# Differential norm: the variance taken inside ScalarE's logarithm and on GpSimd, and the first head's loads spread over slots

## The reference, cut to what matters

```python
def _rmsnorm(x, g):
    y = x * lax.rsqrt(jnp.mean(x * x, axis=-1, keepdims=True) + EPS)
    return y * g

def _diff_attention(q, k, v, lam, lambda_init, g_subln):   # 4 heads, 2048 rows, 64 values
    def block(args):                                       # 128 queries
        qb, t0 = args
        sc = jnp.einsum('bqhmd,bkhmd->bhmqk', qb, k) * scale
        p = jax.nn.softmax(jnp.where(allowed, sc, -jnp.inf), axis=-1)
        a = p[:, :, 0] - lam * p[:, :, 1]
        return jnp.einsum('bhqk,bkhe->bqhe', a, v)
    o = _from_blocks(lax.map(block, (_to_blocks(q), starts)))
    return _rmsnorm(o, g_subln) * (1.0 - lambda_init)
```

## Time and profile before

| | |
|---|---|
| median of three runs | 2027.23 us (2026.43 to 2027.46) |
| the profiled execution | 2035.85 us |
| its span, first to last instruction | 2034.1 us |
| PE / PEld / DVE / ACT / POOL busy | 91% / 77% / 64% / 53% / 30% of the span |
| granted TensorE clock, mean | 0.96 of full speed |
| differential stage | about 1450 us to 1822 us of the span |

### The profile page before, as it was taken

One profiled execution on the slowest core, in us unless ns is written; L12 is line 12 of the kernel. 1 busy time (PEld: TensorE's weight loads), 2 busy tenths in 40 slices (PEclk: granted clock), 3 DMA queues, 4 the chain that ended last, 5 costly groups with the idle time before them and its releaser, 6 DMA issues.

```text
span 2034.1 us, 34303 instructions
## 1 busy us (share of the span) xinstructions
PE 1856.4 (91%) x11552; PEld 1557.3 (77%) x11552; DVE 1305.7 (64%) x2685; ACT 1085.4 (53%) x2406; POOL 603.7 (30%) x542
## 2 busy tenths in 40 slices
PE   6999998889898989898989899999689999979998
PEld 6999998767777777777777787777466666657886
DVE  7705888267676767676767683434577778754454
ACT  6321122266666666666666673434478989962221
POOL 0000000034343434343434350101246666650000
PEclk9999999699999999999999999999599999998999
DMA  6423112200101010101010102413801414016442
GB/s 217 108 68 109 67 67 83 68 6 7 26 5 26 5 26 5 26 5 26 5 26 5 26 18 78 154 53 111 185 1 27 89 27 92 7 54 230 174 145 83
DMA packets 121837, 129.05 MB, mean 63 GB/s; under 512 B 81936, under 2 KB 94992, under 8 KB 120464
## 3 DMA queue, kind: packets, MB, share of 16 engines
q1 hardware_dynamic: 121744, 127.86, 21.6%
HBM read 85.89 MB, written 41.94 MB: 63 GB/s over the span
## 4 chain that ended last, share of the span: by engine, by line
PE 68%; DVE 15%; issue 7%; ACT 6%; POOL 3%; DMA 1%; SPq 0%; DVEq 0%; POOLq 0%; ACTq 0%
PE ps L665 7%; PE ps L619 6%; PE ps L651 5%; PE ps L621 5%; PE ps L620 5%; PE ps L606 4%; PE ps L607 4%; PE ps L608 4%; DVE small L1507 4%; PE ps L897 3%; PE ps L899 3%; PE ps L898 3%; DVE ring L1387 2%; PE ps L848 2%; POOL ring_r L1625 2%
## 5 line engine op out<-in xcount | busy, mean ns | idle before, releaser
L1625 POOL TENSOR_TENSOR ring_r<-ring,sp_hi 128x512 fp32r<-128x512 f32 (+1 forms) x320 | 358.2, 1119 | 855.5 <-DVE sp_hi L1390 855.5
L665 PEld LDWEIGHTS ps<-v,ring 128*128 128x128 f32 x2176 | 284.9, 192 | 52.6 <-issue 17.4
L665 PE MATMUL ps<-v,ring 128*128 128x65 f32 x2176 | 284.9, 270 | 16.3 <-ACT ring L1047 9.8
L1035 ACT ACTIVATE ring<-ps 128x512 f32<-128x512 f32 (+1 forms) x320 | 170.5, 533 | 228.1 <-PE ps L642 135.4
L619 PE MATMUL ps<-ht_hi,w_hl 128*128 128x512 f32 x448 | 199.2, 445 | 25.5 <-DVE sb_s L1417 24.9
L606 PE MATMUL ps<-w_hl,ht_hi 128*128 128x256 f32 x768 | 214.1, 279 | 0.5 <-DVE w_hl L1245 0.3
L607 PE MATMUL ps<-w_hl,ht_hi 128*128 128x256 f32 x768 | 213.9, 279 | 0.0
L608 PE MATMUL ps<-w_hl,ht_lo 128*128 128x256 f32 x768 | 213.9, 278 | 0.0
L1651 POOL TENSOR_TENSOR p<-p 128x1024 f32<-128x1024 f32 (+4 forms) x96 | 164.8, 1728 | 164.6 <-ACT p L1157 164.4
L1387 DVE SCALAR_TENSOR_TENSOR ring<-ring,ps 128x512 f32<-128x512 f32 (+1 forms) x320 | 191.4, 598 | 27.1 <-ACT ring L1040 26.0
L1507 DVE TENSOR_REDUCE small<-ps 128x1 f32<-128x1024 f32 (+4 forms) x192 | 168.7, 905 | 49.3 <-PE ps L806 29.0
(11 more groups left out here) (182 smaller groups left out, 3944.3 us busy)
## 6 DMA issues: line engine op xcount, KB each, us to landing
w_raw<-in_w_narrow SPq DMA_DIRECT2D x18, 512.0 KB, 3.8
xb<-in_x SPq DMA_DIRECT2D x16, 512.0 KB, 4.2
gate_scr<-ring SPq DMA_DIRECT2D x64, 128.0 KB, 1.8
cs<-rot_scr SPq DMA_DIRECT2D x32, 256.0 KB, 3.9
gb<-gate_scr SPq DMA_DIRECT2D x16, 512.0 KB, 3.6
yb<-y_scr SPq DMA_DIRECT2D x16, 512.0 KB, 4.5
xr<-in_x SPq DMA_DIRECT2D x16, 512.0 KB, 4.3
out_y<-ob SPq DMA_DIRECT2D x16, 512.0 KB, 2.9
```

The source lines that it names most:

```text
L665: mm = pe.matmul(ps[:, 4 + i % 2, j * (HD + 1):(j + 1) * (HD + 1)], ring[:, 4 + i % 2, j * P:(j + 1) * P], v1[:, kb, :], start=True, stop= ...
L1625: nc.gpsimd.tensor_tensor(ring_r[:, i % 4, j0 * P:], ring[:, i % 4, j0 * P:], sp_hi[:, i % 4, j0 * P:].bitcast(F32), ALU.subtract).then_in ...
```

## The change

In the differential norm, DVE keeps the sum of squares (L1557) and no longer makes the variance (L1561). ACT's logarithm reads the sum itself, with scale 1/64 and eps as a per-partition bias column (`eps_col`, set once by a DVE memset at the start, behind the semaphore `eps_ok`). POOL makes the variance for the Newton step by a `tensor_scalar` at the head of `df_norm`. The waits move with it: DVE now waits before the sum of batch b until POOL and ACT have read the sum of batch b - 1 (`df_var`, `df_ln`); ACT waits for the sum and for POOL's Newton step of batch b - 1 (`df_nr`); POOL waits for the sum.

On SP, `load_df_v(0)` moves to slot 27, and the four parts of `load_qk(0)` are issued in slots 28 to 31, one part to a slot, so that the stores of memory row steps 26, 27 and 28 stand between them.

```diff
--- before.py
+++ after.py
@@ -154,6 +154,7 @@
         small = sb("small", [P, 256], F32)
         invf = small[:, 0:1]
         minus_lam = small[:, 1:2]
+        eps_col = small[:, 7:8]
         qk_scale = sb("qk_scale", [P, 1], F32)
         w_raw = sb("w_raw", [P, DC * WIDE], F32)
         with ExitStack() as a:
@@ -305,6 +306,7 @@
             sem("df_" + n) for n in ("oc", "ot", "ob", "sq", "ss", "var", "ln", "y0", "nr", "r", "g", "yok"))
         df_pad = [sem("df_pad0"), sem("df_pad1")]
         pool_go = sem("pool_go")
+        eps_ok = sem("eps_ok")
         lam_ch, lam_e = sem("lam_ch"), sem("lam_e")
         wo_in, wo_hi_ok, wo_lo_ok, gpost_in = [sem("wo_in0"), sem("wo_in1")], sem("wo_hi_ok"), sem("wo_lo_ok"), sem("gpost_in")
         o_xr, o_out = ([sem(f"o_{n}{u}") for u in range(2)] for n in ("xr", "out"))
@@ -437,10 +439,12 @@
                 sp.wait_ge(df_lo, f + 1)
                 sp.dma_start(qk_scr[h, 1, :, cols], lo_tmp[:, f % 2, :].bitcast(F32)).then_inc(qk_out[f % 2], 16)
 
-            def load_qk(h):
+            def load_qk(h, only=None):
 
                 u, half = h % 2, S // 2
                 for part, dst, row, first in ((0, df_k, 2 * DQ, 0), (0, df_q, 0, half), (1, df_k, 2 * DQ, half), (2, df_q, 0, 0)):
+                    if only not in (None, (part, row)):
+                        continue
                     cols = slice(first, first + half)
                     for r, hl in enumerate((0, 1, 0) if dst is df_k else (0, 0, 1)):
                         sp.dma_start(dst[u][r * DQ:(r + 1) * DQ, :, cols].bitcast(F32),
@@ -472,12 +476,14 @@
                         store_qk(f)
 
 
+                if slot == X_SLOT[-1] + 2:
+                    load_df_v(0)
                 if slot == X_SLOT[-1] + 3:
                     for u in range(2):
                         sp.wait_ge(qk_out[u], 32 * NT // 2)
                     sp.wait_ge(x_pj, len(X_ITEMS))
-                    load_qk(0)
-                    load_df_v(0)
+                if 3 <= slot - X_SLOT[-1] < 7:
+                    load_qk(0, ((0, 2 * DQ), (0, 0), (1, 2 * DQ), (2, 0))[slot - X_SLOT[-1] - 3])
 
 
             for u in range(2):
@@ -1187,9 +1193,16 @@
             def df_root(s):
                 if s % 2 or not 0 <= s < N_SL:
                     return
-                rsqrt_of(df_tmp(4, 4), df_tmp(8, 4), df_tmp(12, 4), df_var, s // 2 + 1, df_ln, df_y0)
+                b = s // 2
+                act.wait_ge(df_ss, b + 1)
+                if b:
+                    act.wait_ge(df_nr, 4 * b)
+                nc.scalar.activation(df_tmp(8, 4), df_tmp(0, 4), ACT.Ln, scale=1.0 / HD, bias=eps_col).then_inc(df_ln, 1)
+                act.wait_ge(df_ln, b + 1)
+                nc.scalar.activation(df_tmp(12, 4), df_tmp(8, 4), ACT.Exp, scale=-0.5).then_inc(df_y0, 1)
 
             act.wait_ge(m_y, N_MT)
+            act.wait_ge(eps_ok, 1)
             for u in range(2):
                 act.wait_ge(qk_out[u], 32 * len(X_D) // 2)
             for s in range(N_SL + 6):
@@ -1261,6 +1274,7 @@
                 src = (0, 1, 2, 0, 3, 4)[k]
                 nc.vector.tensor_copy(dst[:], cst[:, src, :]).then_inc(const_ok, 1)
             nc.vector.memset(v1[:, :, HD:HD + 1], 1.0).then_inc(lam_ch, 1)
+            nc.vector.memset(eps_col, EPS).then_inc(eps_ok, 1)
             nc.vector.memset(qk_scale[0:2 * DQ, :], -DQ ** -0.5).then_inc(df_scale, 1)
             nc.vector.memset(qk_scale[2 * DQ:P, :], 1.0).then_inc(df_scale, 1)
             lam4 = lam_in.rearrange("p (a b d) -> p a b d", a=2, b=2)
@@ -1552,13 +1566,12 @@
                 if s % 2 or not 0 <= s < N_SL:
                     return
                 b = s // 2
-                ss, var = df_tmp(0, 4), df_tmp(4, 4)
+                ss = df_tmp(0, 4)
                 dve.wait_ge(df_sq, b + 1)
+                if b:
+                    dve.wait_ge(df_var, b)
+                    dve.wait_ge(df_ln, b)
                 nc.vector.tensor_reduce(ss, osq[:], AXX, ALU.add).then_inc(df_ss, 1)
-                dve.wait_ge(df_ss, b + 1)
-                if b:
-                    dve.wait_ge(df_nr, 4 * b)
-                nc.vector.tensor_scalar(var, ss, 1.0 / HD, EPS, ALU.mult, ALU.add).then_inc(df_var, 1)
 
             for u in range(4):
                 dve.wait_ge(m_yout[u], 16 * N_MT // 4)
@@ -1653,8 +1666,10 @@
             def df_norm(b):
                 var, y0, tmp, r = df_tmp(4, 4), df_tmp(12, 4), df_tmp(16, 4), df_tmp(20, 4)
                 a = acc[:, b % 2]
+                pool.wait_ge(df_ss, b + 1)
+                nc.gpsimd.tensor_scalar(var, df_tmp(0, 4), 1.0 / HD, EPS, ALU.mult, ALU.add).then_inc(df_var, 1)
+                pool.wait_ge(df_var, b + 1)
                 pool.wait_ge(df_y0, b + 1)
-                pool.wait_ge(df_var, b + 1)
                 pool.sem_inc(pool_go, 1)
                 nc.gpsimd.tensor_tensor(tmp, y0, y0, ALU.mult).then_inc(df_nr, 1)
                 pool.wait_ge(df_nr, 4 * b + 1)
```

## The result

The change makes the kernel faster: 2012.26 us (2009.79 to 2014.84, five runs) against 2027.46 (2026.43 to 2032.51, five runs). The ratio is 0.9918, with a 95% interval from 0.9904 to 0.9932; 0.0082 of 2027.46 is 16.6 us, where 17.4 was forecast; the two medians lie 15.2 apart. The profiled execution took 2012.26 us, with a span of 2010.2.

The account below looks back on a forecast made before the run. DVE's variance, held behind POOL's instruction, was taken to keep ACT and PE waiting in odd differential iterations. ACT's wait -14.7, clock -3.1, POOL's variance +0.4 sum to -17.4 us: 2027.23 becomes 2009.8, so 2010, range 2002 to 2019.

Parts of the forecast that it names:

- The mechanism: Differential stage: DVE's variance, 0.17 us of work, stands behind POOL's running instruction 14 times, 2.12 us in the median.
- L1561 leaves DVE: Differential stage, odd iterations: removing DVE's variance saves ACT's wait of 1.05 us in each of 14 batches, -14.7 us.
- The lower clock goes with the hole: Two odd iterations at granted clock 0.87 keep 2.4 GHz once the hole goes: 1.55 us each, -3.1 us.
- What takes L1561's place: On DVE, the sum and minima follow at once and no other instruction is held; nothing moves.
- POOL's new variance: POOL's differential norm: 0.38 us more a batch, with room for it; on the path only at stage end, +0.4 us once.
- POOL has the room: POOL, busy 7.23 of 11.2 us in an odd iteration, can take the variance's 0.38 us a batch.
- The logarithm: ACT's logarithm with scale and bias is the same four-column instruction: adds nothing, bounds 0 and 14 x 0.2 us.
- The new waits on DVE: DVE's sum waiting until POOL and ACT have read the previous one: 2.15 us to spare, cost 0.
- Rival D: Slower: DVE's sum waits for a late POOL, 4.7 us late in all 14 batches, +6 us to 2033; chance 0.04.
- The loads: First differential head's loads, spread between memory-row stores on SP: 0 us, the last store's landing staying 1.58 us.
- rival E: Last memory-row store queued behind the fourth load part: up to +4 us, 2014; counted inside the forecast's 0.65 chance.
- The odd iterations: Differential stage: odd iterations take 10.1 to 10.5 us with PE busy nearly throughout; above 10.8 with ACT's waits elsewhere means wrong.
- rival B: Odd iterations: ACT becomes the bound and keeps 0.7 us idle; only -6.3 us, no clock won, 2021; chance 0.13.

Follow-up runs that it names:

- e3: The kernel before the change, with the variance still on DVE but made by four one-column instructions instead of one four-column one; 2011.65 us, ratio 0.9917 to before.
- e4: The changed kernel plus a four-column variance at its old place on DVE, whose result nobody reads; 2026.19 us, ratio 0.9981 to the kernel before.
- e10: The kernel before the change, with ACT's root (logarithm and exponential) moved behind its next exponentials and copy; 2032.76 us, ratio 1.0013 to before.
- e5: The changed kernel without the eps bias column in ACT's logarithm, eps staying in the Newton step; 2012.20 us, ratio 0.9915 to the kernel before.
- e2: The kernel before the change, with only SP's loads spread as in the changed kernel; 2031.14 us, ratio 1.0003 to before.
- e9: The changed kernel, with the memory step's two-column tensor_scalar on DVE made as two one-column instructions; 2011.07 us, ratio 0.9901 to the kernel before.

## Why the prediction was right

**The mechanism was right.** POOL's running instruction holds DVE's four-column `tensor_scalar`. It is taken off (after), made narrow (e3), or put back (e4), and the time follows each time. The Trainium skill (SBUF — State Buffer, Who interferes with whom) says that issue order decides who blocks; the two batches of e4 agree, 0.22 us when DVE is 0.16 ahead and 2.09 when it is 0.28 behind.

**"L1561 leaves DVE", -14.7: the place was wrong, the size nearly right.** The term was priced by ACT's wait for the variance, as the wait that ends last. e10 takes that wait away and wins nothing that helps; e4 gives ACT no such wait and loses the gain again. The price is PE's wait for the copy behind the hold: 17.8 us in 14 batches, 1.27 each, and in e3, which adds only three short instructions on DVE, the eleven odd iterations at full clock fall by 1.31 in the mean. The prediction showed that wait in one batch, 1.39 us, and did not add it up. The two waits differ by 0.2 us a batch, and after does not collect all of the larger one: its stretch is 1.8 us longer than e3's. Of that 0.5 is the bias column (e5); of the rest, 1.0 goes with POOL's longer norm, as the rows under its term show. So two errors, 3.1 too little (17.8 - 14.7) and about 1.8 not taken off, partly cancelled, and that is luck.

**"The lower clock goes with the hole", -3.1: the size nearly right, the reason not shown.** Iterations 9 and 17 took 13.0 us at 0.87 before, and take 10.10 and 10.80 at 1.00; PE's busy time in these two windows falls by 1.64 and 1.66 us, 3.3 of the 4.42 in the stretch. By the stretch's own bounds the two fell by 2.92 and 2.11 us, the other eleven odd ones by 1.17 in the mean, so the clock gave back some 2.7 us, not 3.1. But a hole does not bring the low clock by itself. In before, ten other odd iterations were held for 1.85 to 2.36 us and none of them was at the low clock; the prediction compared with the one short hole alone. In e10 s = 9 and 17 have the same two waits of PE as before in their first six microseconds, 0.34 us and then 1.26 or 1.27, and run at 1.00. In e4 the clock falls in s = 11 and 19 in place of 9 and 17. All ten profiles without the 14 or 9 holds have the full clock over the whole stretch, so the change did win this term; what decides whether a held iteration loses the clock stays open.

**What takes L1561's place: nothing, right.** The sum keeps its 0.42 us, and all 64 of L1541, one column each, take 0.263 to 0.274 us, as in the earlier trace rows.

**POOL's new variance, +0.38 a batch and +0.4 at the end: right there, but it costs elsewhere too.** The chain at the end of the stage, to be laid beside the earlier trace rows:

```profile
1792.40 2.35 POOL p L1664
...
1794.83 0.20 POOL small L1670
...
1796.68 0.62 POOL acc L1690
...
1798.23 0.33 SPq L525
```

From the variance to the first Newton instruction, 1795.23, it is 0.40 us; from the end of the difference to SP's store 3.48 against 2.95 (1821.28 - 1818.33). "POOL has the room" was read from an average. Late in s = 13 and 19 POOL runs without a pause: the norm, then the weight split, then the next difference, which therefore reaches PE later. PE's turn in s = 13, in after and then in e3, where DVE makes the variance:

```profile
1600.21 0.66 PE L838 MATMUL ps<-ident,p 128*128 128x128 f32 x4 [0.79 <-POOL p L1664]
```

```profile
1599.49 0.66 PE L832 MATMUL ps<-ident,p 128*128 128x128 f32 x4 [0.28 <-POOL p L1653]
```

In s = 13 and 19 after is 0.51 us longer than e3 each, and stays so in e5: 1.0 us that the sum did not have.

**The logarithm, 0 within 0 to 2.8: inside the bounds, not zero.** It is not the same instruction, but one with a column operand: 0.303 against 0.210 us. The Trainium skill (ScalarE: Activation LUTs, What ACT_TABLE_LOAD costs) gives about 93 ns for such an operand, which these rows bear out; the prediction priced the instruction without its column.

**The new waits on DVE, 0: right.** One batch in the stage waited, 0.2 us for POOL's variance. Rival D would have needed more than 4 us of lateness.

**The loads, 0: right** (e2, 1.0003). SP's queue and the chain after:

```profile
1427.06 1.31 SPq L450 DMA_DIRECT2D df_k<-qk_scr  x3
1428.60 0.36 SPq L469 DMA_DIRECT2D y_scr<-acc  x1
1429.00 1.43 SPq L450 DMA_DIRECT2D df_q<-qk_scr  x3
...
1437.83 1.57 SPq L450 DMA_DIRECT2D df_q<-qk_scr  x3
1441.77 4.63 SPq L469 DMA_DIRECT2D y_scr<-acc  x3
```

```profile
1446.07 1.57 DMA y_scr<-acc
```

The parts stand between the stores as forecast, and the last landing takes 1.57 us against 1.58; rival E did not happen.

**The odd iterations, 10.1 to 10.5 us: right in the mean, not one by one.** The 13 average 10.40 but run from 9.85 to 10.97. Four of them, 5, 11, 17 and 23, are at or above 10.8, a sign of being wrong only together with waits of ACT, and it has none there; all four have a weight split. ACT, busy for 99% of s = 9 and s = 17, is what fills those two. That is rival B's half truth: ACT is the bound there, but it does not keep the idle time that B priced at 0.7 us each.

**The total.** -14.7 - 3.1 + 0.4 = -17.4 against -16.6 by the runs and -17.55 in the stretch. The hold's removal was worth more than its term, the clock a little less, and the column and POOL's norm cost what the sum had at nothing.

## What to carry to other kernels

Group one line's instructions and look for a maximum or median far above the minimum: 0.17 us of work that takes 2.1 beside a busy POOL is a hold, and splitting it into single columns or moving it by two places (with ACT's root moved too) won as much here as moving the work to other engines. Price such a hold by the engine that bounds the stage: find the first instruction behind it, in its own queue, for which that engine waits, and add up that wait, not the one that is named with the held line. In e4 that wait and the time lost agree, 9.4 us each. When the hold is gone, look at which engine now fills the iteration, and move its optional work (here a weight split) to where it idles.

## What the runs showed of the hardware that was not expected

- The hold depends on the form: `tensor_scalar` on four columns took up to 2.36 us and on two up to 6.12 beside POOL, on one column, with constants, 0.141 to 0.155 in all 128 of e3 and e9, 62 of which ran wholly inside a POOL instruction.
- In the differential stage of before a held instruction ended with the POOL instruction that ran when it started, 0.02 to 0.03 us after it in all 14 batches.
- A POOL instruction that only writes, the zero fill, holds DVE too, and whether DVE gets in between two fills in a row differs from one execution to the next: 6.1 us in two profiles, 2.4 to 2.7 in nine others with the same DVE and POOL code there.
- A column as the bias of a four-column logarithm costs 0.093 us.
- Equal holes do not bring an equal clock: with the same waits of PE in s = 9 to 0.01 us, the clock was 0.87 in before and 1.00 in e10.
- Taking a wait off one line of ACT moved all of it, 14.7 us, to the next exponential, 16.8 us (e10), with no gain.
